# Hyena transforms folded by parity, heads in alternating order, keys and values projected ahead of queries

## The reference

```python
def fft_long_conv(u, k, d):
    l = u.shape[1]
    uf = u.astype(jnp.float32)
    uk = jnp.fft.rfft(uf, n=2 * l, axis=1) * jnp.fft.rfft(k, axis=0)[None]
    y = jnp.fft.irfft(uk, n=2 * l, axis=1)[:, :l]
    return (y + uf * d.astype(jnp.float32)).astype(u.dtype)

def hyena_mixer(h_hy, short_w, short_b, w1, b1, w2, b2, w3, b3, w4, freq, bias_d):
    u = depthwise_conv(h_hy, short_w, short_b)
    v, x1, x2 = jnp.split(u, HY_ORDER + 1, axis=-1)
    k = hyena_filters(h_hy.shape[1], w1, b1, w2, b2, w3, b3, w4, freq)
    z = x1 * fft_long_conv(v, k[:, 0], bias_d[0])
    return x2 * fft_long_conv(z, k[:, 1], bias_d[1])
```

## Time and profile before

| | us |
|---|---|
| three runs | 3616.07, 3629.35, 3634.42 (median 3629.35) |
| the profiled execution | 3617.26 |
| its span in the trace | 3615.5 |
| PE busy | 3373.7 (93%) |
| DVE, ACT, POOL busy | 1788.5, 757.2, 1970.1 |
| mean granted PE clock | 0.974 |

### The profile page before, as it was taken

How to read it: one execution, slowest core, us unless ns; L and a number is a source line. 1 busy time by engine, 2 the same in 40 slices (tenths; PEclk the granted TensorE clock), 3 DMA queues, 4 the chain that set the end, 5 groups by cost and what they waited for, 6 DMA issues and landing times.

```text
span 3615.5 us, 44996 instructions
## 1 busy us (share of the span) xinstructions
PE 3373.7 (93%) x14544; PEld 2626.5 (73%) x14544; DVE 1788.5 (49%) x1990; ACT 757.2 (21%) x1269; POOL 1970.1 (54%) x1148
## 2 busy tenths in 40 slices
PE   7999998889999999998889999889988999999997
PEld 5888774368887788875447888667766777778886
DVE  6532266463312743147545331566668776853313
ACT  2110124422211111012432220111122222222201
POOL 4446654346666645666416666534444455666664
PEclk9999999999999999999899999999999999999998
DMA  4223320023333322331002333312222122233332
GB/s 149 71 75 94 112 86 12 7 64 95 96 95 120 100 59 88 95 114 42 12 18 88 98 93 96 104 58 66 70 62 63 60 71 70 87 93 94 99 93 76
DMA packets 77138, 284.07 MB, mean 79 GB/s; under 512 B 9350, under 2 KB 9734, under 8 KB 75848
## 3 DMA queue, kind: packets, MB, share of 16 engines
q1 hardware_dynamic: 74016, 268.84, 24.8%
q10 hardware_dynamic: 2984, 13.41, 1.1%
HBM read 280.12 MB, written 2.10 MB: 78 GB/s over the span
## 4 chain that ended last, share of the span: by engine, by line
PE 77%; DVE 16%; issue 4%; ACT 2%; DVEq 0%; ACTq 0%; DMA 0%; SPq 0%
PE bank L540 22%; PE bank L545 22%; PE bank L544 22%; PE bank L663 2%; PE bank L809 1%; PE bank L745 1%; PE bank L791 1%; DVE xbc L2085 1%; DVE x_lo L1606 1%; PE bank L735 1%; DVE y L1839 1%; PE bank L800 1%; DVE scaled L1916 1%; DVE short L1788 1%; DVE ssm_lo L1751 1%
## 5 line engine op out<-in xcount | busy, mean ns | idle before, releaser
L440 POOL TENSOR_SCALAR w_hi<-raw 128x1024 fp32r<-128x1024 f32 x504 | 551.4, 1094 | 1560.2 <-PE bank L540 1551.5
L443 POOL TENSOR_TENSOR w_lo<-raw,w_hi 128x1024 fp32r<-128x1024 f32 x504 | 1267.7, 2515 | 42.0
L540 PE MATMUL bank<-x_hi,w_hi 128*128 128x512 f32 x2896 | 1156.5, 399 | 77.0 <-DVE x_lo L1606 30.3
L544 PE MATMUL bank<-x_lo,w_hi 128*128 128x512 f32 x2896 | 1139.2, 393 | 0.0
L545 PE MATMUL bank<-x_hi,w_lo 128*128 128x512 f32 x2896 | 1138.7, 393 | 0.0
L540 PEld LDWEIGHTS bank<-x_hi,w_hi 128*128 128x128 f32 x2896 | 551.2, 190 | 218.7 <-issue 89.3
L544 PEld LDWEIGHTS bank<-x_lo,w_hi 128*128 128x128 f32 x2896 | 551.6, 190 | 118.6 <-issue 5.1
L545 PEld LDWEIGHTS bank<-x_hi,w_lo 128*128 128x128 f32 x2896 | 550.5, 190 | 117.1
L545 PE MATMUL bank<-hidden_hi,w_lo 128*128 (+1 forms) x880 | 347.6, 395 | 0.0
L540 PE MATMUL bank<-hidden_hi,w_hi 128*128 (+1 forms) x880 | 347.6, 395 | 0.0
L544 PE MATMUL bank<-hidden_lo,w_hi 128*128 (+1 forms) x880 | 347.6, 395 | 0.0
(11 more groups left out here) (323 smaller groups left out, 3466.7 us busy)
## 6 DMA issues: line engine op xcount, KB each, us to landing
raw<-in_w SPq DMA_DIRECT2D x504, 512.0 KB, 3.6
dft<-in_dft ACTq DMA_DIRECT2D x2, 2048.0 KB, 8.8
x<-in_x SPq DMA_DIRECT2D x2, 1024.0 KB, 6.5
filt_cos<-in_dft ACTq DMA_DIRECT2D x2, 1024.0 KB, 7.9
filt_sin<-in_dft ACTq DMA_DIRECT2D x2, 1024.0 KB, 10.6
out<-x SPq DMA_DIRECT2D x4, 512.0 KB, 2.6
mask<-in_mask ACTq DMA_DIRECT2D x1, 1536.0 KB, 7.4
sel<-in_sel ACTq DMA_DIRECT2D x1, 768.0 KB, 4.7
```

The source lines that it names most:

```text
L440: nc.gpsimd.tensor_scalar(w_hi[:, s % 2, :], raw[:, s, :], 1.0, 0.0, ALU.mult, ALU.add).then_inc(w_rounded, 1)
L443: nc.gpsimd.tensor_tensor(w_lo[:, s % 2, :], raw[:, s, :], w_hi[:, s % 2, :].bitcast(F32), ALU.subtract).then_inc(w_split, 1)
L540: first = nc.tensor.matmul(out, hi_w, hi, start=start, stop=False)
L544: nc.tensor.matmul(out, hi_w, lo, start=False, stop=False)
```

## The change

Tokens and frequencies are split into even and odd. A spectrum is computed at 256 of the 512 frequencies, once over even and once over odd tokens (`frequencies(o, k)`, k = 0, 1: even tokens in one PSUM bank, odd in the other); sum and difference of the two give both halves of the spectrum. The inverse gives 256 even and 256 odd tokens from the sum and the difference of the halves. The number of PE units per transform so falls from four to two, on the filters' side too. In exchange ACT copies the odd bank to SBUF (`odd_half`), DVE adds and subtracts (`fold`, `filter_spectrum`), and `spectrum_product` becomes eight multiplications, four sums of 256 columns and two of 512, all with both inputs in SBUF. The tables of ACT's loads shrink (1024 to 512 KB twice and 2048 to 1536 KB per layer). `y_update` reads and writes with a stride of two. Further: `mla_inputs` projects keys and values ahead of queries; `head` on PE runs its first unit ahead of the turns, DVE runs it after the second maximum, and ACT alternates exponentials and copies; the sums of a head are inverted ahead of the second unit; the query ropes of successive heads are interleaved; the centring of the convolution is unchanged but comes behind the sums of head 7.

```diff
@@ frequencies, PE
+                for parity in range(2):
+                    for part in range(2):
+                        for a in range(2):
+                            last = nc.tensor.matmul(bank[HYENA_BANKS[parity]][:, part * CW:(part + 1) * CW],
+                                                    dft[:, parity, part, a, k * P:(k + 1) * P],
+                                                    v_time[:, 2 * parity + a, :], start=a == 0, stop=a == 1)
                 last.then_inc(freq_ready, 1)
...
@@ inverse, PE
+            def inverse(o, i):
+
+                after(out_spec_ready, 2 * o + 2)
+                for parity in range(2):
+                    for k in range(2):
+                        for part in range(2):
+                            at = part * CW + i * P
+                            last = nc.tensor.matmul(bank[HYENA_BANKS[i]][:, parity * CW:(parity + 1) * CW],
+                                                    out_spectrum[:, parity, k, at:at + P],
+                                                    dft[:, 2 * parity, part, k, :], start=k == 0 and part == 0,
+                                                    stop=k == 1 and part == 1)
+                last.then_inc(convolved, 1)
...
@@ mla_inputs, PE: behind keys and values
+                s = take()
+                for h in range(4):
+                    if h >= 2:
+                        after(k_copied, 2 * g + h - 1)
+                    for k in range(2):
+                        last = product(bank[QUERY_BANKS[h]][:], s, 2 * h + k, latent_hi[k], latent_lo[k],
+                                       k == 0, k == 1)
+                    last.then_inc(q_ready, 1)
...
@@ head, PE
                 if h == 3:
                     mla_inputs(1)
                     first_unit()
+                    first_scores(h + 1)
                     mla_inputs_taken(1)
                     turn(h, 0)
                     turn(h, 1)
-                    scores(h + 1, 0)
-                    scores(h + 1, 1)
-                    scores(h + 1, 2)
                 else:
                     if h < 7:
                         scores(h + 1, 0)
                         scores(h + 1, 1)
                         scores(h + 1, 2)
+                    first_unit()
                     turn(h, 0)
                     turn(h, 1)
-                    first_unit()
                 if h < 7:
...
@@ mixer, PE
-                frequencies(0, 1)
                 pe.wait_ge(tile_free, c.at(tile_free) + len(RING))
                 mla_inputs(0)
-                frequencies(0, 2)
+                frequencies(0, 1)
+                first_scores(0)
                 mla_inputs_taken(0)
-                scores(0, 0)
-                scores(0, 1)
-                scores(0, 2)
-                frequencies(0, 3)
                 scores(0, 3)
-                inverse(0, 0, 0)
-                head(0, lambda: inverse(0, 0, 1), lambda: inverse(0, 1, 0))
-                head(1, lambda: inverse(0, 1, 1), nothing)
+                head(0, nothing, lambda: inverse(0, 0))
+                head(1, lambda: inverse(0, 1), nothing)
                 head(2, lambda: signal_transposes(1), lambda: frequencies(1, 0))
-                head(3, lambda: frequencies(1, 1), lambda: frequencies(1, 2))
-                head(4, lambda: frequencies(1, 3), lambda: inverse(1, 0, 0))
-                head(5, lambda: inverse(1, 0, 1), lambda: inverse(1, 1, 0))
-                head(6, lambda: inverse(1, 1, 1), conv_mean)
+                head(3, lambda: frequencies(1, 1), nothing)
+                head(4, nothing, lambda: inverse(1, 0))
+                head(5, lambda: inverse(1, 1), nothing)
+                head(6, nothing, conv_mean)
...
+                def odd_half(k):
+                    act.wait_ge(freq_ready, c.next(freq_ready))
+                    nc.scalar.activation(fold_tiles[k][1], bank[HYENA_BANKS[1]][:], ACT.Copy
+                                         ).then_inc(odd_copied, 1)
...
@@ head, ACT
-                    else:
-                        for t in range(3):
-                            exponential(h + 1, t)
-                        turned(h, 0)
-                        turned(h, 1)
+                        turned(h, 2)
+                        exponential(h + 1, 3)
+                        turned(h, 3)
+                        return
+                    for t in range(2):
+                        exponential(h + 1, t)
+                        turned(h, t)
                     if between is not None:
                         between()
-                    exponential(h + 1, 3)
-                    turned(h, 2)
-                    turned(h, 3)
+                    for t in range(2, TT):
+                        exponential(h + 1, t)
+                        turned(h, t)
...
+                def fold(o, k):
+                    dve.wait_ge(odd_copied, c.next(odd_copied))
+                    even, (low, odd) = bank[HYENA_BANKS[0]][:], fold_tiles[k]
+                    nc.vector.tensor_tensor(low, even, odd, ALU.add)
+                    nc.vector.tensor_tensor(odd, even, odd, ALU.subtract
+                                            ).then_inc(spec_free, c.add(spec_free))
+                    tap()
                     dve.wait_ge(spec_free, c.at(spec_free))
+
+                def spectrum_product(o, k):
+
+                    def terms(to, *pairs):
+                        for product, (a, b) in zip(to, pairs):
+                            last = nc.vector.tensor_tensor(product, a, b, ALU.mult)
+                        last.then_inc(dve_step, c.add(dve_step))
+                        return c.at(dve_step)
+
+                    first = [products[:, n, :] for n in range(4)]
+                    second = [*halves(key_rope), *halves(mix_rms)]
+                    low, high = fold_tiles[k]
+                    (re, im), (f_re, f_im) = halves(low), halves(spectrum[:, k, o, :])
+                    first_made = terms(first, (re, f_re), (im, f_im), (re, f_im), (im, f_re))
+                    (im, re), (f_re, f_im) = halves(high), halves(spectrum[:, 2 + k, o, :])
+                    second_made = terms(second, (im, f_re), (re, f_im), (re, f_re), (im, f_im))
+                    dve.wait_ge(dve_step, first_made)
+                    nc.vector.tensor_tensor(low[:, 0:CW], first[0], first[1], ALU.subtract)
+                    nc.vector.tensor_tensor(low[:, CW:], first[2], first[3], ALU.add)
+                    dve.wait_ge(dve_step, second_made)
+                    nc.vector.tensor_tensor(high[:, 0:CW], second[0], second[1], ALU.subtract)
+                    nc.vector.tensor_tensor(high[:, CW:], second[2], second[3], ALU.add
+                                            ).then_inc(dve_step, c.add(dve_step))
+                    made = c.at(dve_step)
+                    tap()
+                    dve.wait_ge(dve_step, made)
+                    nc.vector.tensor_tensor(out_spectrum[:, 0, k, :], low, high, ALU.add)
+                    nc.vector.tensor_tensor(out_spectrum[:, 1, k, :], low, high, ALU.subtract
+                                            ).then_inc(out_spec_ready, c.add(out_spec_ready))
...
@@ DVE
                 def head(h, first_unit, second_unit=nothing):
                     if h == 3:
-                        query_ropes()
+                        query_ropes(True)
                         first_unit()
-                    for t in range(3):
-                        maximum(h + 1, t)
+                    maximum(h + 1, 0)
+                    maximum(h + 1, 1)
                     if h != 3:
                         first_unit()
-                    if h == 3:
-                        second_unit()
+                    maximum(h + 1, 2)
                     maximum(h + 1, 3)
-                    if h != 3:
-                        second_unit()
                     invert_sums(h + 1)
+                    second_unit()
                     mixed(h)
...
@@ mixer, DVE
-                head(0, lambda: y_update(0, 0))
-                head(1, first_done)
-                head(2, nothing, lambda: spectrum_product(1, 0))
-                head(3, lambda: spectrum_product(1, 1), lambda: spectrum_product(1, 2))
-                head(4, lambda: spectrum_product(1, 3))
-                head(5, lambda: y_update(1, 0))
+                def hyena_done():
+                    y_update(1, 1)
+                    dve.sem_inc(norm_in, 1)
+
+                head(0, lambda: spectrum_product(0, 1))
+                head(1, lambda: y_update(0, 0), first_done)
+                head(2, nothing, lambda: fold(1, 0))
+                head(3, nothing, lambda: spectrum_product(1, 0))
+                head(4, lambda: fold(1, 1), lambda: spectrum_product(1, 1))
+                head(5, lambda: y_update(1, 0), hyena_done)
```

More of the change, by code:

```diff
@@ L759, in mla_inputs @@
                 s = take()
-                for h in range(4):
-                    for k in range(2):
```

(20 more changed lines are left out.)

215 lines of the change are left out of this document (114 added, 101 removed).

## The result

The changed kernel takes 3579.28 us (median of 4 runs, 3573.93 to 3581.65) against 3628.14 for the kernel before in the same comparison; the ratio is 0.9867, interval 0.9839 to 0.9895. Forecast were 3588 and a range from 3555 to 3616. The span of the profiled execution fell from 3615.5 to 3572.1 us, 43.4 less; the forecast gain was 34.

The account below looks back on a forecast made before the run. PE was taken to bound the filter stage, while DVE's queue stood behind most attention waits. Savings of 27.7 and 6.4 us made 34: 3583 from the profiled execution, 3595 from the median, 3588 named between, range 3555 to 3616.

Parts of the forecast that it names:

- Filters, -27.7: Filter stage, both layers: half the PE units save 13.8 us per layer, 27.7 together; DVE's additions cost nothing.
- Attention, -3.2 per layer: Mixer attention: a ledger of six stretches in one layer sums to -3.2 us, doubled to -6.4 for both.
- A product beside the convolution: Spectrum product on DVE while POOL convolves: 6.4 us undisturbed plus 14 x 0.4 for contention, 12.0 us.
- head 4: Head 4, 17.6 us and full: product (1,0) and DVE work queued behind it lengthen it to 36.0, +18.4.
- product (1,1): Spectrum product in head 4, behind the convolution: 8 us of DVE with its tap, ahead of the inverse unit.
- The 2.2 us for PE at a lower clock: Part of head 4's sum: 2.2 us for PE restarting at a lower clock.
- Product (0,1) only at its start, taken as 9: Heads 0 and 1: product meets the convolution only at its start, 9 us, 6 covered; stretch changes by -0.4.
- The opening's +3.4: Attention's opening, 48.0 us, set by DVE: folds and products add 4.4 us, pipelined ropes drop 1.0, +3.4.
- Of 27.7 us of PE work 24.5 come back as waits: One layer's attention: PE work falls by 27.7 us, but waits return 24.5, leaving -3.2.
- Hidden contention: Rival, attention: products run at undisturbed 6.4 us, -19 per layer instead of -3.2, 3556 in all; chance 0.15.
- Strictly taking turns: Rival, attention: every DVE instruction waits for POOL, product 20.4 us, +10.8 per layer, 3616, no change; chance 0.18.
- The clock: Rival, attention: PE's mean clock falls; 0.84 costs 17 us per layer, 0.75 costs 35, giving 3658; chance 0.03.

Follow-up runs that it names:

- run 3: Changed kernel with the matmuls of each filter spectrum issued twice: 3600.1 us, ratio 0.9922.
- run 9: The combined kernel: changed kernel with queries projected first, products with one input in PSUM, and POOL's first convolution stretch held back: 3546.1 us, ratio 0.9791.
- run 12: The combined kernel, with ACT also copying the latent tiles before the first spectrum's odd half instead of behind it: 3537.9 us, ratio 0.9767.
- run 6: Changed kernel with queries projected ahead of keys and values again, pipelined ropes kept: 3570.5 us, ratio 0.9836.
- Run 4: Changed kernel with the matmuls of frequencies and inverse issued twice in the mixers: 3624.5 us, ratio 0.9988.
- run 1: Changed kernel without 27 of the 30 convolution taps POOL computes per mixer, output not the reference's: 3538.9 us, ratio 0.9754.
- run 2: Kernel before without the same POOL convolution taps, output not the reference's: 3614.1 us, ratio 0.9967.
- run 5: Changed kernel with ACT's order of before, three exponentials and then two copies of turned probabilities: 3615.9 us, ratio 0.9963.
- run 10: Kernel before with only ACT's alternation of exponentials and copies of turned probabilities added: 3626.8 us, ratio 0.9998.
- run 11: Changed kernel with ACT's order of before and DVE's first unit behind the third maximum instead of the second: 3604.1 us, ratio 0.9941.
- run 8: Changed kernel with sum and difference of the spectra written back to PSUM, second frequency units moved later: 3566.0 us, ratio 0.9823.

## Why the prediction came out as it did

*Filters, -27.7: right.* The spans ahead of the two attentions shrank by 16.2 and 11.4 us, 27.6 together, and run 3 gives 24.6 of it back by the spans, 21 by the medians. The mechanism is shown; that it came out to a tenth is chance. The start of the first mixer lies within 506 and 514 us over the executions of the changed kernel and its variants, so the split between 16.2 and 11.4 means nothing.

*Attention, -3.2 per layer: right in direction, in one layer in size.* The first layer gave 3.8. The second gave 10.6, because the kernel before took 207.8 us there; I had doubled the first layer's ledger instead of cutting the second one, where head 3 took 41.2 us and the opening 49.0. That the first layer came within 0.6 us is partly luck: the opening was 4.8 us worse than forecast, heads 0 and 1 3.5 and heads 3 and 4 1.0 each better. Of the 9 us by which the span's gain exceeded the forecast, 7.4 are the second layer's attention.

*The sizes of the terms.* A product beside the convolution was taken at 12.0 us, its tap of 1.0 apart, and takes 13.2 with the tap; head 4 came out +17.4 for +18.4, though not in all its parts: product (1,1), taken as 8 with its tap, ran from 656.06 to 661.58, 5.5 us without one, while 11.1 us of product (1,0) and not 10 lay inside the head. The 2.2 us for PE at a lower clock came as 2.5, an inverse unit of 5.99 us for 3.46. "Product (0,1) only at its start, taken as 9" was wrong: POOL had finished at 557 us, and it takes 5.9, which is why heads 0 and 1 gave 3.9 instead of 0.4. The opening's +3.4 was mis-sized most, +8.2. "DVE sets this stretch" let me leave out what comes ahead of DVE: ACT's copy of the odd half ahead of the latent tiles, worth 3.3 to 3.6 us of opening (runs 9 and 12, on the combined kernel), and keys and values first, 3.5 to 4.7 us (run 6, where the first rope starts 13.3 us behind the transposes for 17.2). I had counted only 3.1 us for it, in head 3. The two make more than the 4.8 us missing; the ledger of the opening was not closed.

*"Of 27.7 us of PE work 24.5 come back as waits": the sum holds, the reading of it fails.* It suggested that PE's work in the mixers is worth little. Run 4 puts its price at 23 of 27.7 us: PE and DVE mostly work one after the other, so both count. What offsets it is the work of DVE, of which 18 to 19 us per layer come from POOL alone (run 1; the kernel before paid 0 to 7, run 2), and 4 for the new order of projections. And the alternation of ACT, of which I had booked under 2 us, is worth 15 us per layer in the presence of the rest and nothing alone (runs 5, 10). Part of it is that it keeps a product between two maxima from stopping the mixes; without that product it was still worth 8 to 11 (run 11).

*The rivals.* Hidden contention: the runs at 5.9 us exist, but only beside an idle POOL; run 1, where taps and folds lose their share as well, bounds it: 3539 where I had named 3556. Strictly taking turns: 13.2 us is far from 20.4. The four sums took 0.82, 1.48, 0.41 and 0.82 us: DVE waits for POOL at some of its instructions, not at each. The clock: the granted clock over the first attention fell from 0.94 to 0.84, exactly where this rival let 17 us per layer eat the gain, and the attention still was 3.8 us shorter. It is low in the stretches in which PE waits for DVE, 0.70 and 0.71, and 1.00 in heads 5 to 7. I had multiplied all 139 us of PE work by it. PE was busy 145.5 us where the halved work at the old clock would be 139: some 6 us, partly on the path, as the inverse unit in head 4 shows, and as may be so in heads 0 and 1, where PE was busy 27.7 of 28.7 us at 0.86. By these figures, an estimate since the ends of matmuls are modelled, the clock cost at most some 6 us per layer and not 17; it was not measured apart.

## What to carry to other kernels

Halving products on the busiest engine by additions on another one is a trade: price the other engine's part with its neighbour at work, and look where its operands lie. An operand that stays in PSUM may be worth more than the instruction count; here it was 3 us for a product beside POOL and nothing for one beside an idle POOL.

When a long unit is put into a strict queue, write down what stands behind it on that engine and which copies stand behind that on the next. The alternation was worth nothing in the kernel before and 15 us per layer in the changed one, and moving the unit back explained only a part of that, so parts of a change can't be priced one by one.

A low clock in a stretch that waits anyway costs less than the whole work times the ratio of the clocks; multiply by it only the work that is on the path.

## What was not expected of the hardware

A DVE instruction of 256 columns with both inputs in SBUF took 0.42 us beside an idle POOL, with a start every 0.33 to 0.34 us, and 0.41 to 1.48 us beside POOL's convolution; eight multiplications took 5.9 and 6.6 us there and 2.7 with one input in PSUM, as beside an idle POOL. POOL pays too: 1.00 for 0.69 us and 1.42 for 1.27. Writing sum and difference back into PSUM banks cost DVE nothing that the trace shows: 0.70 and 0.69 us in run 8, 0.69 and 0.68 in the changed kernel.
